# A state-space scan whose third quarter of pairs moves from VectorE to GpSimd

## The chip, the cores and the metric

The kernel runs on one core of one Trainium2 chip. The time is the device time of one execution in microseconds (us). The engines named here are TensorE (PE in the profile; PEld is its weight load), VectorE (DVE), ScalarE (ACT), GpSimd (POOL) and SyncE (SP), which issues the loads of the weights.

## The reference

Two blocks run one after the other on 256 tokens of width 2048. The second has two layers; each has a mixer, a cross attention and a feed-forward part of 8192. The change is in the mixer of its second layer, a state-space model. Cut to what matters:

```
def s5_mixer(u, lam_re, lam_im, log_dt, b_re, b_im, c_re, c_im, d_skip, w_glu, b_glu):
    lam_bar = jnp.exp(lam * dt)                       # 128 groups x 64 complex states
    def chunk_step(state, u_c):
        bu = jnp.einsum('bcgi,gpi->bcgp', u_c, b_bar)  # the input of every state
        bu = bu.at[:, 0].add(lam_bar * state)
        _, states = lax.associative_scan(combine, (a_elem, bu), axis=1)
        y = jnp.einsum('bcgp,gip->bcgi', states, c_mat).real
        return states[:, -1], y
    ...
    y = y + d_skip * uf
    z = jax.nn.gelu(y)
    return z * jax.nn.sigmoid(z @ w_glu + b_glu)
```

The mixer's input is `xn @ odd_w_in` and its result is multiplied by `odd_w_out`; both matrices and `w_glu` are 2048 x 2048.

## The kernel before

**Weights.** All large products stream their weights through a ring of 8 slots (`RING`), each 256 rows by 512 columns. For a slot, SyncE loads the raw fp32 values, ScalarE rounds them (`round_hi`, L1840: high part), VectorE subtracts (`take_lo`, L2790: low part), and TensorE takes three products for each tile (high x high, high x low, low x high; `gemm`, L988). A product waits for the counter `w_lo` of its slot, so VectorE has to keep up with the slots in the order of the program. A step of the ring is 12 matmuls. In the scan phase, `low(c, s)` is the low part for the slot eight places behind slot s of chunk c of `odd_in`; `low(3, s)` thus serves the first eight slots of the next product, `glu`.

**The scan.** The 256 tokens are taken four at a time, which leaves 64 positions. The tile `s_h` holds, on 128 partitions, 64 positions x real and imaginary x 64 pairs. The product `odd_in` makes u in four chunks (c = 0 to 3). For each, TensorE turns u (`turn_u`, L1691) and multiplies it with the input matrix (`drive`, L1707), and ScalarE copies the result into `s_h` (`driven`, L2603), which raises `bu_ready`. Chunk c gives the pairs 16c to 16c + 15. The 64 positions are scanned as 8 segments of 8: seven steps q advance all segments together (four VectorE instructions each: two products into the scratch tile `prob_t`, two additions into `s_h`), then seven steps s carry the end of one segment into the next (five instructions each). So a scan has 14 steps and 63 instructions, whatever the number of pairs. `scan(k)` is a generator that stops after each step, and its caller puts other work there. VectorE scans the pairs 0 to 15, then 16 to 31 (both on pieces of 256 elements for each partition), then 32 to 63 in one go (512 elements).

**What follows.** `scanned()` raises `scan_done` after the second scan and after the third. TensorE runs `taps` (L1733, L1739) first, which needs the tile `s_T`; GpSimd issues the four DMAs for `s_T` and two for `s_C` (L686, queue of POOL) when `odd_in` has ended. Then `read_half(0)` (L1760) waits for the first `scan_done`; ScalarE applies gelu (L2664), TensorE turns the result (`turn_z`, L1771), ScalarE copies and rounds it (L2647, L2652) and VectorE makes its low part (`z_lo`, L4132). `unread(8)` (L932) are 8 products that nobody reads. The product `glu` begins with the k range of this first half: four slots of column chunk 0, four of chunk 1. It waits for `feat_part`, which `z_lo(1)` and `z_lo(3)` raise. After its sixth slot comes `read_half(1)`, which waits for the second `scan_done`.

**Order.** The order on every engine is written by hand; each engine runs its own list from front to back. GpSimd has little work besides DMA issues and three additions on gate vectors (L762).

The line of every VectorE instruction of the scan is that of its helper, L4054.

Of the kernel before, what the change touches and what calls it, by code (L numbers as in the profile page):

```python
# [36 lines left out]
P = 128  # L37
# [4 lines left out]
CH = 512  # L42
# [12 lines left out]
PAIRS = 64  # L55
# [140 lines left out]
def two_blocks(nc, I, out):  # L196
    ctx = ExitStack()
    with ctx:
        sems = {}

        def sem(name):
            if name not in sems:
                sems[name] = ctx.enter_context(nc.semaphore(name))
            return sems[name]
# [54 lines left out]
        prob_t = sb("prob_t", [P, 2, 4, P])  # L259
# [19 lines left out]
        s_cd = dram("s_cd", (4, P, 2048))  # L279
        s_td = dram("s_td", (4, P, 1024))  # L280
# [67 lines left out]
        gemms = defaultdict(list)  # L348
# [115 lines left out]
        def groups_done(last):  # L464

            done = 0
            for st in ORDER:
                for g in gemms[st]:
                    done += g.n * g.tiles
                    if g is last:  # L470
                        return done
# [94 lines left out]
        s_T = view(4096, 32, 2, S5_STEP, 16)  # L566
        s_C = [view(o, S5_STEP, 2, 16, 16) for o in (24576, 26624, 8192, 10240)]
        s_h = view(12288, NM, 2, PAIRS)
        s_l2 = stage[:, 0, 256:512].rearrange("p (z c k) -> p z c k", z=2, c=2)
        rstd_s = stage[:, 1, 0:TT]  # L570
        S5_RUN = 8
        S5_SEGS = NM // S5_RUN
        s_pw = prob[:, :, :].rearrange("p z (r k) -> p z r k", k=PAIRS)
# [107 lines left out]
        def _(pool):  # L681
            L = Eng(pool, sem, "pool_step")

            def dma(dst, src, name):
                with nc.allow_non_contiguous_dma(reason="small constant"):
                    pool.dma_start(dst, src).then_inc(sem(name), 16)  # L686
# [28 lines left out]
            dma(x4_b1[:, 0:2], I["x"][0].rearrange("(t p) d -> p t d", p=P), "x_in")  # L715
            dma(x4_b1[:, 2:4], I["ctx"][0].rearrange("(t p) d -> p t d", p=P), "x_in")

            def flat4(v):
                return v.rearrange("p a b c d -> p (a b c d)") if len(v.shape) == 5 else v.rearrange("p a b c -> p (a b c)")

# [14 lines left out]
            for l in range(2):  # L735
                if l == 0:
                    for n, item in enumerate(b1_items[0]):
                        if item[0] == "in" and item[2] >= 6:
                            c = item[2] - 6
# [37 lines left out]
            for c in MIX:  # L777
                cs, b = mix_cols(c), c % 2
                n = cs.stop - cs.start
# [75 lines left out]
            for l in range(2):  # L855
                if l == 0:
                    pool.wait_ge(sem("mem_free"), L.due("mem_free"))
                    for j in range(2):
                        pool.wait_ge(sem(f"kv_out{j}"), 16 * 4)
                else:  # L860
                    pool.wait_ge(sem("s5_free"), L.due("s5_free"))
                    dma(s_l2.rearrange("p z c k -> p (z c k)"), s_ld2, "b_in0")
                    for j in range(2):
                        dma(flat4(s_B[j]), s_bd[j], f"b_in{j // 2}")
                    pool.wait_ge(sem("x_normed"), L.due("x_normed"))
                    dma(x_d.rearrange("(t p) d -> p t d", p=P), x4, "x_out")
                    pool.wait_ge(sem("x_out"), 32)
                    pool.wait_ge(sem("u_ready_s5"), L.due("u_ready_s5"))
                    for j in range(2, 4):
                        dma(flat4(s_B[j]), s_bd[j], f"b_in{j // 2}")  # L870
                    pool.wait_ge(sem("bu_ready"), L.due("bu_ready", 2))
                    for j in range(2):
                        dma(flat4(s_C[j]), s_cd[j], "c_in0")
                    pool.wait_ge(sem("gemm_full"), groups_done(gemms["odd"][0]))
                    for j in range(4):
                        dma(s_T[:, 8 * j:8 * j + 8].rearrange("p a b c d -> p (a b c d)"), s_td[j], "t_in_s5")
                    for j in range(2, 4):
                        dma(flat4(s_C[j]), s_cd[j], "c_in1")
                    pool.wait_ge(sem("s5_done"), L.due("s5_done"))
                    dma(x4, x_d.rearrange("(t p) d -> p t d", p=P), "dve_load")  # L880
                dma(xa_kv, kv_d[l].rearrange("(t p) d -> p t d", p=P), "mem_in")
# [932 lines left out]
        def _(act):  # L1814
# [761 lines left out]
            def odd():  # L2576
# [14 lines left out]
                def ut_in(c):  # L2591
                    for g in range(2):
                        f(s_ut[:, 8 * c:8 * c + 8, g], take_turn()[:, :].rearrange("p (n m) -> p n m", m=NM), ACT.Copy) \
                            .then_inc(sem("act_tp"), E.up("act_tp"))
                    act.wait_ge(E.last_sem(), E.last_count())
                    act.nop().then_inc(sem("ut_ready"), E.count("ut_ready"))

                def driven(c):
                    for n0 in (0, 4):
                        for o in range(2):  # L2600
                            n = 8 * c + n0
                            dst = s_h.rearrange("p m z (n o) -> p o n z m", o=2)[:, o, n:n + 4, :, 1:NM]
                            f(dst, take_turn()[:, :].rearrange("p (n z m) -> p n z m", z=2, m=NM)[:, :, :, 0:NM - 1], ACT.Copy) \  # L2603
                                .then_inc(sem("act_tp"), E.up("act_tp"))
                    act.wait_ge(E.last_sem(), E.last_count())
                    act.nop().then_inc(sem("bu_ready"), E.count("bu_ready"))
# [13 lines left out]
                def s5_ahead(c, s):  # L2620
                    if (c, s) in ((1, 3), (2, 1), (3, 1)):
                        ut_in(c - 1)
                    if (c, s) in ((1, 5), (2, 3), (3, 3)):
                        driven(c - 1)
                    if (c, s) == (2, 5):
                        for t in range(TT):
                            u_out(2, None, t, take("gemm_full"))
                    if (c, s) == (3, 6):
                        ut_in(3)
                    if (c, s) == (3, 4):  # L2630
                        for t in range(TT):
                            u_out(3, None, t, take("gemm_full"))
# [3 lines left out]
                        u_out(c, None, t, take("gemm_full"))  # L2636

                stream(g_in, u_chunk, unroll=True, each=s5_each, ahead=s5_ahead)
                driven(3)
                nonlocal g_n  # L2640
                y_at = g_n
                g_n += 4
# [72 lines left out]
        def _(dve):  # L2715
# [296 lines left out]
            def mark(name):  # L3012
                dve.wait_ge(E.last_sem(), E.last_count())
                dve.nop().then_inc(sem(name), E.count(name))
# [1025 lines left out]
            def odd():  # L4040
# [9 lines left out]
                def after(n=0):  # L4050
                    dve.wait_ge(sem("dve_step"), E.cnt["dve_step"] - n)

                def step(out, a, b, op):
                    tt(out, a, b, op).then_inc(sem("dve_step"), E.up())  # L4054

                def powers():
                    for z in range(2):
                        dve.tensor_copy(s_pw[:, z, 0], s_l2[:, z, 0]).then_inc(sem("dve_step"), E.up())
                    n = 1
                    while n < S5_RUN:  # L4060
                        after()
                        have, more = s_pw[:, :, 0:n], s_pw[:, :, n:2 * n]
                        re, im = (s_pw[:, z, n - 1].unsqueeze(1).unsqueeze(1).to_broadcast([P, 2, n, PAIRS]) for z in range(2))
                        part = prob_t[:, :, :, :].rearrange("p a b c -> p a (b c)")[:, :, 0:n * PAIRS].rearrange("p z (r k) -> p z r k", k=PAIRS)
                        step(more, have, re, ALU.mult)
                        step(part, have, im, ALU.mult)
                        after()
                        step(more[:, 0], more[:, 0], part[:, 1], ALU.subtract)
                        step(more[:, 1], more[:, 1], part[:, 0], ALU.add)
                        n *= 2  # L4070
# [37 lines left out]
                        low(c, s)  # L4108
                dve.wait_ge(sem("b_in0"), 48)
                powers()  # L4110
                nonlocal g_n, t_n
                skip("gemm_full", g_in.n * g_in.tiles)
                turn_skip(1 + 4 * 6)
# [14 lines left out]
                def z_lo(j):  # L4128
                    dve.wait_ge(sem("hi_ready"), E.due("hi_ready"))
                    ks = slice(2 * j, 2 * j + 2)  # L4130
                    name = "feat_part" if j % 2 else "dve_step"
                    tt(s_z.lo[:, ks], s_z.raw[:, ks], s_z.hi[:, ks], ALU.subtract).then_inc(sem(name), E.up(name))  # L4132

                for n, _ in enumerate(scan(slice(2 * quarter, PAIRS))):
                    if n in (1, 2):
                        low(3, n + 3)
                    if n in (7, 8):
                        z_lo(2 * n - 14)
                        z_lo(2 * n - 13)
                scanned()  # L4140
                for s in (6, 7):
                    low(3, s)
# [119 lines left out]
```

## Time and profile before

| | us |
|---|---|
| median of 3 runs | 3807.45 (3805.14 to 3809.78) |
| the profiled execution's own time | 3810.78 |
| its span, first to last instruction | 3808.8 |
| TensorE busy | 3705.3 (97%) |
| VectorE busy | 2485.9 (65%) |
| ScalarE busy | 1632.4 (43%) |
| GpSimd busy | 151.8 (4%) |

Times inside the profile count from the span's start. Busy shares are averages over all stages. The scan lies between 2752 and 2853 us. "Waits" name the engine that waited, and behind the arrow what ended its wait. The granted clock of TensorE is 1.00 at 2.4 GHz and 0.50 at 1.2 GHz; in a stretch between these it changed within it.

### The profile page before, as it was taken

To read this page: it belongs to the slowest core of one execution; us is meant where nothing else is said; L and a number is where in the kernel's file an instruction comes from. 1 tells how busy PE (TensorE), PEld (TensorE's weight loads), DVE (VectorE), ACT (ScalarE), POOL (GpSimd) and SP (SyncE) were. 2 spreads that over 40 slices of the span, in tenths; PEclk is the share of its full clock that TensorE was granted. 3 is DMA by queue.
4 is the path that set the end of the run, shared out by engine and by line. 5 is a ranking of instruction groups with operands and counts; after the bars stand their busy time and mean duration, and the time that the engine had idled before them with its cause. 6 is when DMAs were issued, how large, how long until landed. Compare 5 with 4: busy or idle time off the path is not lost.

```text
span 3808.8 us, 50649 instructions
## 1 busy us (share of the span) xinstructions
PE 3705.3 (97%) x20767; PEld 2997.6 (79%) x20767; DVE 2485.9 (65%) x3635; ACT 1632.4 (43%) x2323; POOL 151.8 (4%) x244
## 2 busy tenths in 40 slices
PE   6999999999999999999999999999989999999998
PEld 3688887787887888556888888888878888888887
DVE  7877786577776666667765645655595566545654
ACT  4422233424435443523454434444545554434443
POOL 2000000000000011022000000000000000000000
PEclk8999999999999999999999999999989999999999
DMA  9666564255863577344646656655645656556664
GB/s 376 255 210 205 184 204 170 78 177 167 270 204 111 182 244 211 103 159 145 199 153 189 192 193 189 192 191 191 237 155 162 217 156 190 192 193 189 191 204 155
DMA packets 352582, 722.46 MB, mean 190 GB/s; under 512 B 24064, under 2 KB 26436, under 8 KB 347488
## 3 DMA queue, kind: packets, MB, share of 16 engines
q1 hardware_dynamic: 331872, 637.74, 52.7%
q0 software_dynamic: 18784, 79.22, 6.0%
q8 instruction: 165, 2.70, 0.3%
q10 hardware_dynamic: 1696, 2.26, 0.2%
q14 instruction: 65, 0.53, 0.0%
HBM read 689.34 MB, written 26.37 MB: 188 GB/s over the span
## 4 chain that ended last, share of the span: by engine, by line
PE 88%; DVE 5%; DMA 3%; ACT 2%; issue 1%; POOL 1%; SPq 0%; DVEq 0%; ACTq 0%; POOLq 0%
PE acc L988 57%; PE acc L1523 6%; PE tp L1523 6%; PE acc L1521 3%; PE tp L1521 3%; PE acc L1220 3%; DMA ring<-in_w_mod 2%; PE tp L1038 2%; PE acc L1593 1%; PE acc L1093 1%; DVE big L4054 1%; DVE prob_t L4054 1%; PE acc L1076 1%; DVE ring_r L2790 1%; PE acc L906 0%
## 5 line engine op out<-in xcount | busy, mean ns | idle before, releaser
L2790 DVE TENSOR_TENSOR ring_r<-ring,ring_r 128x1024 fp32r<-128x1024 f32 (+1 forms) x984 | 1188.1, 1217 | 970.5 <-ACT ring_r L1840 959.5
L1840 ACT ACTIVATE ring_r<-ring 128x1024 fp32r<-128x1024 f32 (+1 forms) x984 | 1030.0, 1054 | 1556.9 <-DMA ring<-in_ffn_down 386.6
L988 PE MATMUL acc<-ring_r,feat_hi 128*128 128x512 f32 x2688 | 832.9, 391 | 5.2 <-DVE ring_r L2790 5.2
L988 PE MATMUL acc<-ring_r,hid_t_hi 128*128 128x512 f32 x2048 | 630.8, 389 | 0.0
L988 PEld LDWEIGHTS acc<-ring_r,feat_hi 128*128 128x128 f32 x2688 | 504.1, 188 | 116.2 <-DVE ring_r L2790 6.6
L988 PE MATMUL acc<-ring_r,feat_lo 128*128 128x512 f32 x1344 | 524.6, 390 | 0.0
L988 PEld LDWEIGHTS acc<-ring_r,hid_t_hi 128*128 128x128 f32 x2048 | 384.3, 188 | 79.3
L988 PE MATMUL acc<-ring_r,hid_t_lo 128*128 128x512 f32 x1024 | 398.4, 389 | 0.0
L1523 PE MATMUL acc<-feat_pair,ring_r 128*128 128x512 f32 x1080 | 378.9, 394 | 0.0
L1523 PE MATMUL tp<-feat_pair,ring_r 128*128 128x512 f32 x960 | 337.1, 395 | 0.0
L1521 PE MATMUL acc<-feat_pair,ring_r 128*128 128x256 f32 x1152 | 309.7, 279 | 0.3
L988 PEld LDWEIGHTS acc<-ring_r,feat_lo 128*128 128x128 f32 x1344 | 253.0, 188 | 53.3
L1521 PE MATMUL tp<-feat_pair,ring_r 128*128 128x256 f32 x1024 | 274.0, 278 | 0.0
L988 PE MATMUL acc<-ring_r,feat_e_hi 128*128 128x512 f32 (+1 forms) x832 | 247.9, 381 | 2.0 <-DVEq L2867 2.0
L1523 PEld LDWEIGHTS acc<-feat_pair,ring_r 128*128 128x128 f32 x1080 | 202.5, 188 | 43.4
L988 PEld LDWEIGHTS acc<-ring_r,hid_t_lo 128*128 128x128 f32 x1024 | 192.2, 188 | 40.1
L1521 PEld LDWEIGHTS acc<-feat_pair,ring_r 128*128 128x128 f32 x1152 | 216.5, 188 | 6.8 <-issue 0.7
L1523 PEld LDWEIGHTS tp<-feat_pair,ring_r 128*128 128x128 f32 x960 | 180.1, 188 | 39.6
L1521 PEld LDWEIGHTS tp<-feat_pair,ring_r 128*128 128x128 f32 x1024 | 192.4, 188 | 5.7
L2774 DVE SCALAR_TENSOR_TENSOR big<-ring,silu_c,big 128x512 f32<-128x512 f32 x255 | 177.4, 746 | 28.8 <-DMA ring<-in_w_mod 27.7
L988 PEld LDWEIGHTS acc<-ring_r,feat_e_hi 128*128 128x128 f32 x832 | 153.3, 188 | 32.0 <-issue 2.5
L988 PE MATMUL acc<-ring_r,feat_e_lo 128*128 128x512 f32 (+1 forms) x416 | 158.3, 381 | 0.0
(541 smaller groups left out, 4194.5 us busy)
## 6 DMA issues: line engine op xcount, KB each, us to landing
ring<-in_ffn_up SPq DMA_DIRECT2D x256, 512.0 KB, 3.7
ring<-in_ffn_down SPq DMA_DIRECT2D x256, 512.0 KB, 3.6
ring<-in_w_mod SPq DMA_DIRECT2D x192, 512.0 KB, 4.9
ring<-in_w_in SPq DMA_DIRECT2D x176, 512.0 KB, 4.0
ring<-in_w_out SPq DMA_DIRECT2D x64, 512.0 KB, 3.7
ring<-in_even_w_in SPq DMA_DIRECT2D x64, 512.0 KB, 4.5
ring<-in_xattn_wkv SPq DMA_DIRECT2D x32, 512.0 KB, 4.4
ring<-in_even_w_out SPq DMA_DIRECT2D x32, 512.0 KB, 4.2
```

What stands on the lines that cost most here:

```text
L988: mm = pe.matmul(bank[0:l.shape[-1], 0:width], l, r, start=(kk == 0 and j == 0), stop=(kk == g.kt - 1 and j == len(terms) - 1))
L1038: mm = pe.transpose(bank[0:b.shape[-1], j * P:j * P + b.shape[0]], b, ident[0:b.shape[0], 0:b.shape[0]])
L1076: pe.matmul(bank[:, 0:u["k"].shape[-1]], u["q"], u["k"], start=True, stop=True) \
L1093: mm = pe.matmul(bank[:, 0:HD], prob_t[:, (i - 2) % 2, j, :], v, start=(j == 0), stop=(j == len(u["v"]) - 1))
L1220: mm = pe.matmul(bank[:, :], mem_feat(kk)[:, t * P:(t + 1) * P], ring[:, slot, 1, k, :], start=(kk == 0), stop=(kk == g.kt - 1))
L1521: mm = pe.matmul(bank[:, 0:SEQ], w_lo, feat.hi[:, kk, :], start=False, stop=False)
L1523: mm = pe.matmul(bank[:, :], w_hi, feat_hl[:, kk, :], start=False, stop=kk == g.kt - 1)
L1593: mm = pe.matmul(x_banks[c, t][:, :], x, w, start=(kk == 0 and j == 0), stop=(kk == g_o.kt - 1 and j == 2))
L1840: f(ring_r[:, slot, 0, 0:kt, 0:width], ring[:, slot, 1, 0:kt, 0:width], ACT.Copy) \
L2774: op = stt(v, w, by, v, ALU.mult, ALU.add)
L2790: tt(lo, raw, hi, ALU.subtract).then_inc(sem("w_lo"), E.up("w_lo"))
L4054: tt(out, a, b, op).then_inc(sem("dve_step"), E.up())
```

## The change

GpSimd gets a scan of its own, with the same 14 steps, for the pairs 32 to 47. It uses the upper half of `prob_t` as scratch; VectorE uses the lower. It starts when the third `bu_ready` and the new counter `powers_ready` are there. Its DMA issues for `s_T` and the second half of `s_C`, which stood behind a wait for the end of `odd_in`, now stand behind the second of its steps. VectorE's last scan covers only the pairs 48 to 63, on pieces of 256 elements; the calls of `z_lo` in it move from steps n = 7 and 8 to n = 8 and 10, and before `scanned()` it waits for all 63 GpSimd instructions. ScalarE's `driven(3)` moves ahead of the rounding of the last slot of `odd_in`.

```
@@ gpsimd
+            def step(out, a, b, op):
+                pool.tensor_tensor(out, a, b, op).then_inc(sem("pool_step"), L.up())
+
+            def after(n=0):
+                pool.wait_ge(sem("pool_step"), L.cnt["pool_step"] - n)
+
+            def scan(k):
+                w = k.stop - k.start
+                by_run = s_h.rearrange("p (s r) c k -> p s r c k", r=S5_RUN)
+                tmp = [prob_t[:, z].rearrange("p a b -> p (a b)")[:, CH // 2:].rearrange("p (n c k) -> p n c k", n=S5_RUN, c=2)
+                       for z in range(2)]
+                for q in range(1, S5_RUN):
+                    if q > 1:
+                        after()
+                    last, h = by_run[:, :, q - 1, :, k], by_run[:, :, q, :, k]
+                    for z in range(2):
+                        step(tmp[z], last, s_l2[:, z, :, k].unsqueeze(1).to_broadcast([P, S5_SEGS, 2, w]), ALU.mult)
+                    after(1)
+                    step(h, h, tmp[0], ALU.add)
+                    after()
+                    step(h, h, tmp[1][:, :, ::-1], ALU.add)
+                    yield
...
@@ gpsimd, layer 1
-                    pool.wait_ge(sem("gemm_full"), groups_done(gemms["odd"][0]))
-                    for j in range(4):
-                        dma(s_T[:, 8 * j:8 * j + 8].rearrange("p a b c d -> p (a b c d)"), s_td[j], "t_in_s5")
-                    for j in range(2, 4):
-                        dma(flat4(s_C[j]), s_cd[j], "c_in1")
+                    pool.wait_ge(sem("bu_ready"), L.due("bu_ready"))
+                    pool.wait_ge(sem("powers_ready"), L.due("powers_ready"))
+                    for n, _ in enumerate(scan(slice(PAIRS // 2, 3 * PAIRS // 4))):
+                        if n == 1:
+                            pool.wait_ge(sem("gemm_full"), groups_done(gemms["odd"][0]))
+                            for j in range(4):
+                                dma(s_T[:, 8 * j:8 * j + 8].rearrange("p a b c d -> p (a b c d)"), s_td[j], "t_in_s5")
+                            for j in range(2, 4):
+                                dma(flat4(s_C[j]), s_cd[j], "c_in1")
@@ scalar
+                    if (c, s) == (3, 7):
+                        driven(3)
...
                 stream(g_in, u_chunk, unroll=True, each=s5_each, ahead=s5_ahead)
-                driven(3)
@@ vector
                 powers()
+                mark("powers_ready")
...
-                for n, _ in enumerate(scan(slice(2 * quarter, PAIRS))):
+                for n, _ in enumerate(scan(slice(3 * quarter, PAIRS))):
                     if n in (1, 2):
                         low(3, n + 3)
-                    if n in (7, 8):
-                        z_lo(2 * n - 14)
-                        z_lo(2 * n - 13)
+                    if n in (8, 10):
+                        z_lo(n - 8)
+                        z_lo(n - 7)
+                dve.wait_ge(sem("pool_step"), 4 * (S5_RUN - 1) + 5 * (S5_SEGS - 1))
                 scanned()
```

In the order of the instructions this is seen at two places. GpSimd before, from the first half of `s_C` (`s_cd`) to the load of x behind the mixer (`big` is the large tile that holds `s_T`, `s_C` and `s_h`):

```order
L686 DMA big<-s_cd 128x2048 [waits bu_ready]
L686 DMA big<-s_cd 128x2048
L686 DMA big<-s_td 128x1024 [waits gemm_full]
L686 DMA big<-s_td 128x1024 x3
L686 DMA big<-s_cd 128x2048 x2
L686 DMA big<-x_d 128x2x2048 [waits s5_done]
```

GpSimd after the change, from the same place to the third of its 14 steps (the other eleven follow; L719 is the new helper, `stage` holds the coefficients):

```order
L686 DMA big<-s_cd 128x2048
L719 TENSOR_TENSOR prob_t<-big,stage 128x256 [waits powers_ready,bu_ready]
L719 TENSOR_TENSOR prob_t<-big,stage 128x256
L719 TENSOR_TENSOR big<-big,prob_t 128x8x2x16 [waits pool_step] x2
L719 TENSOR_TENSOR prob_t<-big,stage 128x256 [waits pool_step]
L719 TENSOR_TENSOR prob_t<-big,stage 128x256
L719 TENSOR_TENSOR big<-big,prob_t 128x8x2x16 [waits pool_step] x2
L686 DMA big<-s_td 128x1024 [waits gemm_full]
L686 DMA big<-s_td 128x1024 x3
L686 DMA big<-s_cd 128x2048 x2
L719 TENSOR_TENSOR prob_t<-big,stage 128x256 [waits pool_step]
```

Eight additions and products now stand ahead of the loads of `s_T` (`s_td`), and 55 behind the loads.

VectorE before, from the first step of the last scan that carries a segment over to the second pair of `z_lo` (L4132):

```order
L4054 TENSOR_TENSOR prob_t<-prob,big 128x512 x2
L4054 TENSOR_TENSOR big<-big,prob_t 128x16x32
L4054 TENSOR_TENSOR big<-big,prob_t 128x8x32 x2
L4132 TENSOR_TENSOR s_zlo<-big,s_zhi 128x512 x2
L4054 TENSOR_TENSOR prob_t<-prob,big 128x512 x2
L4054 TENSOR_TENSOR big<-big,prob_t 128x16x32
L4054 TENSOR_TENSOR big<-big,prob_t 128x8x32 x2
L4132 TENSOR_TENSOR s_zlo<-big,s_zhi 128x512 x2
```

VectorE after the change, from the same step (the lines are 42 or 43 higher):

```order
L4096 TENSOR_TENSOR prob_t<-prob,big 128x256 x2
L4096 TENSOR_TENSOR big<-big,prob_t 128x16x16
L4096 TENSOR_TENSOR big<-big,prob_t 128x8x16 x2
L4096 TENSOR_TENSOR prob_t<-prob,big 128x256 x2
L4096 TENSOR_TENSOR big<-big,prob_t 128x16x16
L4096 TENSOR_TENSOR big<-big,prob_t 128x8x16 x2
L4175 TENSOR_TENSOR s_zlo<-big,s_zhi 128x512 x2
```

The pieces are half as long, and the first pair of `z_lo` stands one step later.

## Rows read from the trace of the kernel before

**Rows 1.** The page, part 4: engines in the chain that ended last.

```profile
PE 88%; DVE 5%; DMA 3%; ACT 2%; issue 1%; POOL 1%; SPq 0%; DVEq 0%; ACTq 0%; POOLq 0%
```

**Rows 2.** The page, part 1: busy time of TensorE and VectorE.

```profile
PE 3705.3 (97%) x20767; PEld 2997.6 (79%) x20767; DVE 2485.9 (65%) x3635; ACT 1632.4 (43%) x2323; POOL 151.8 (4%) x244
```

**Rows 3.** Waits of PE, 2740 to 2900: us in total, times, longest.

```profile
PE acc L988 <- DVE s_zlo L4132: 5.5, 1, 5.5
PE acc L1733 <- DMA big<-s_td: 4.1, 1, 4.1
```

**Rows 4.** Timeline of PE: start, duration, instruction, count [idle before].

```profile
2812.13 9.60 PE L1760 MATMUL acc<-big 64*64 64x64 f32 x256
...
2824.22 1.97 PE L1771 MATMUL acc<-ident,big 64*128 64x64 f32 x16 [1.34 <-ACTq L2669]
2826.12 3.78 PE L932 MATMUL acc<-ident 128*128 128x128 f32 x16
2835.40 1.19 PE L988 MATMUL acc<-ring_r,s_zhi 128*128 128x512 f32 x2 [5.51 <-DVE s_zlo L4132]
...
2840.66 0.75 PE L988 MATMUL acc<-ring_r,s_zhi 128*128 128x512 f32 x2
...
2854.52 9.64 PE L1760 MATMUL tp<-big 64*64 64x64 f32 x256
```

**Rows 5.** Busy time and granted clock (behind POOL's) in stretches.

```profile
2831.00:2835.00 4.00, 0.00 (x0) 0.00 (x0) 3.93 (x8) 0.25 (x1) 0.00 (x0) 0.50 0.00 0
...
2841.00:2843.00 2.00, 2.00 (x10) 1.63 (x9) 1.97 (x5) 0.00 (x0) 0.00 (x0) 1.00 0.45 125
```

**Rows 6.** Timeline of DVE, from the second scan to the end of the third.

```profile
2783.38 0.75 DVE L4054 TENSOR_TENSOR prob_t<-big,stage 128x256 f32<-128x256 f32 x2
2784.05 0.88 DVE L4054 TENSOR_TENSOR big<-big,prob_t 128x256 f32<-128x256 f32 x2
2784.96 0.76 DVE L4054 TENSOR_TENSOR prob_t<-big,stage 128x256 f32<-128x256 f32 x2
...
2794.49 0.76 DVE L4054 TENSOR_TENSOR prob_t<-prob,big 128x256 f32<-128x256 f32 x2
...
2806.20 4.63 DVE L2790 TENSOR_TENSOR ring_r<-ring,ring_r 128x1024 fp32r<-128x1024 f32 x4
2810.75 1.28 DVE L4054 TENSOR_TENSOR prob_t<-big,stage 128x512 f32<-128x512 f32 x2
...
2833.97 1.29 DVE L4132 TENSOR_TENSOR s_zlo<-big,s_zhi 128x512 fp32r<-128x512 f32 x2
...
2852.70 8.05 DVE L2790 TENSOR_TENSOR ring_r<-ring,ring_r 128x1024 fp32r<-128x1024 f32 x7
```

**Rows 7.** Groups of DVE by shape, 2783.3 to 2852.7: busy us, mean ns.

```profile
L4054 DVE TENSOR_TENSOR prob_t<-big,stage 128x512 f32<-128x512 f32 x14 | 9.0, 686 | 0.1
L4054 DVE TENSOR_TENSOR prob_t<-big,stage 128x256 f32<-128x256 f32 x14 | 5.3, 420 | 0.2
```

**Rows 8.** Timeline of ACT.

```profile
2780.30 3.88 ACT L2603 ACTIVATE big<-tp 128x504 f32<-128x504 f32 x4
...
2800.95 3.59 ACT L2603 ACTIVATE big<-tp 128x504 f32<-128x504 f32 x4
...
2827.32 0.63 ACT L2652 ACTIVATE s_zhi<-big 128x512 fp32r<-128x512 f32 x1
```

**Rows 9.** Timeline of POOL, around 2790.

```profile
2791.56 2.09 POOL L686 DMA_DIRECT2D big<-s_td  x4 [32.53 <-PE acc L988]
2793.64 1.05 POOL L686 DMA_DIRECT2D big<-s_cd  x2
```

**Rows 10.** Groups of POOL: busy us, mean ns.

```profile
L762 POOL TENSOR_TENSOR big<-big 128x2048 f32<-128x2048 f32 x3 | 13.5, 4521 | 14.8 <-DMA big<-in_b_mod 14.8
```

**Rows 11.** Timeline of DVE before and during a GpSimd addition (663.3 to 672.3).

```profile
661.75 0.35 DVE L2971 SCALAR_TENSOR_TENSOR big<-acc,att_s,big 128x128 f32<-128x128 f32 x1 [0.38 <-PE acc L1093]
...
666.13 0.35 DVE L2971 SCALAR_TENSOR_TENSOR big<-acc,att_s,big 128x128 f32<-128x128 f32 x1 [0.38 <-PE acc L1093]
```

More of the change, by code:

```diff
@@ L716, in _ @@
             dma(x4_b1[:, 2:4], I["ctx"][0].rearrange("(t p) d -> p t d", p=P), "x_in")
+            def step(out, a, b, op):
[18 more added lines that the diff above has]
+                    yield
+                shape = [P, S5_RUN, 2, w]
+                for s in range(1, S5_SEGS):
+                    after()
+                    end, h = by_run[:, s - 1, S5_RUN - 1, :, k].unsqueeze(1).to_broadcast(shape), by_run[:, s, :, :, k]
+                    for z in range(2):
+                        step(tmp[z], s_pw[:, z, :, k].unsqueeze(2).to_broadcast(shape), end, ALU.mult)
+                    after(1)
+                    step(h, h, tmp[0], ALU.add)
+                    after()
+                    step(h[:, :, 0], h[:, :, 0], tmp[1][:, :, 1], ALU.subtract)
+                    step(h[:, :, 1], h[:, :, 1], tmp[1][:, :, 0], ALU.add)
+                    yield
+                after()
             def flat4(v):
```

## The prediction, made before the changed kernel ran

> **What bounds the kernel now.** I read part 4 of the page first, the chain that ended last. TensorE holds 88% of it and VectorE 5% [rows 1], and TensorE is busy 97% of the span [rows 2]. So the change is worth what it takes from TensorE's idle time or adds to it; VectorE's 65% decide nothing by themselves.
>
> The waits of TensorE in the scan phase come next [rows 3]. It waits twice: 4.1 us for the load of `s_T`, and 5.5 us for `s_zlo`, the low part by VectorE. The timelines show why the second is there. ScalarE begins the second rounding at 2827.32 and needs 0.63 us [rows 8], so both operands of `z_lo(1)` are there at 2827.95. TensorE ends its unread products at 2826.12 + 3.78 = 2829.90. But VectorE is inside the scan of 32 pairs and comes to `z_lo` only at 2833.97 [rows 6]; TensorE starts `glu` at 2835.40 [rows 4]. The idle time also costs clock: the granted clock is 0.50 in 2831 to 2835 and 1.00 from 2841 [rows 5]. The first 12 matmuls of `glu` take 2840.66 - 2835.40 = 5.26 us [rows 4]. The 60 that follow up to 2854.52 take 13.86 us, 0.23 us each, at which pace 12 take 2.8 us. So this place costs up to 5.5 + 2.5 = 8.0 us, and that is all that a faster scan can give: `read_half(1)` follows at 2854.52 without a wait, because the second `scan_done` is there at 2852.7 [rows 4, 6]. Behind it TensorE is full, and what is gained or lost at `glu` reaches the end one for one.
>
> **What is removed.** VectorE's third scan works on 512 elements for each instruction, 0.686 us; on 256 it is 0.420 us [rows 7]. That gives 0.266 us for 256 elements (1.04 ns each) and 0.154 us that doesn't depend on the size. A q step on 256 elements takes 2784.96 - 2783.38 = 1.58 us, an s step 1.66 (2794.49 and the next; the second scan ends at 2806.20, seven steps after 2794.49, which is 1.67) [rows 6]. The last scan begins at 2810.75 either way. After the change `z_lo(1)` would be done behind 7 x 1.58 + 2 x 1.66 + two `low` of 4.63 / 4 = 1.15 + two `z_lo` of 0.65: 11.1 + 3.3 + 2.3 + 1.3 = 18.0 us, so at 2828.8, before TensorE wants it at 2829.9. The scan itself ends after five more s steps and two more `z_lo`, 9.6 us, at 2838.4. TensorE would come to `read_half(1)` at 2854.52 - 8.0 = 2846.5.
>
> **What is added.** 63 GpSimd instructions, 49 on 256 elements and 14 on 128. The trace has GpSimd additions only on 2048 elements: 4.521 us, 2.2 ns for an element [rows 10]. In proportion, 256 elements cost 0.565 us; with VectorE's fixed 0.154 us, 0.72. I take 0.72 (and 0.44 for the short ones), because a short instruction has a start too: 49 x 0.72 + 14 x 0.44 = 41.4 us. GpSimd starts when the third `driven` ends, 2780.30 + 3.88 = 2784.2 [rows 8]; `powers_ready` is long there. With 3.1 us of DMA issues [rows 9] it ends at 2828.8, 17.7 us before TensorE asks. It would be late only above (2846.5 - 2784.2 - 3.1) / 63 = 0.94 us for an instruction.
>
> **The moved DMA issues.** The loads of `s_T` go behind eight GpSimd instructions: 2784.2 + 8 x 0.72 = 2790.0, and they waited for the end of `odd_in` until 2791.56 anyway [rows 9]. Nothing at 0.72; at 0.94 us the loads start 0.2 us late, and TensorE's wait for `s_T` grows by as much. The 2 issues for `s_C` are needed at 2854 only. The long queue on GpSimd behind them holds `dma(x4)` after the mixer, which is far away.
>
> **The new wait on VectorE.** Behind the wait for the 63 instructions stand `scan_done`, `low(3, 6)`, `low(3, 7)` and the lows of `glu`. TensorE needs these only after `read_half(1)`, 9.64 us long [rows 4], and before the change they also started at the end of the scan [rows 6]. So only the time of `scan_done` matters.
>
> **ScalarE.** `driven(3)` before the last rounding (about 1 us) ends at about 2802.5 in place of 2804.5 [rows 8]. VectorE asks for it at 2810.75 [rows 6], `low(3, 7)` later still. Nothing.
>
> **The disputed cost: both engines on SBUF at once.** If they run freely, the sum is -5.5 - 2.5 = -8.0 us. But from 2784.2 on VectorE has hardly a gap, and every instruction of both reads two operands from SBUF. The only overlap in this trace is with softmax work: a VectorE instruction that reads PSUM and one SBUF tile takes 0.35 us both before and inside a GpSimd addition [rows 11]. That is no slowdown, but it isn't this pair: there VectorE reads one operand from SBUF. So the cost is bounded by free overlap and by full exclusion, where an instruction of one holds the other back. By exclusion in turns, only the data parts excluding each other, a pair of long instructions takes 0.266 + 0.565 = 0.83 us, a short pair 0.42. VectorE has 61 of the 63 instructions of its second scan left at 2784.2, 47 long and 14 short, 0.74 us for an average pair. Eight run beside the DMA issues (3.1 us), 53 in pairs: 39 us. The first `scan_done` comes at 2826.4 in place of 2806.2. Four `low` (4.6 us) lose 2.3 us to the next four GpSimd instructions, the last scan 3 us to the remaining six: `z_lo(1)` ends at 2826.4 + 6.9 + 18.0 + 3.0 = 2854.3, and `glu` starts 19.0 us later than before, with `read_half(1)` not late. With whole durations excluding each other (0.35 + 0.66 = 1.01 us for a pair) the same sum gives +33. If VectorE always goes first, its chain keeps its times and GpSimd is starved: between packed data parts without a gap (VectorE 96 x 0.266 + 28 x 0.133 for the scans + 6 x 1.06 for `low` + 4 x 0.53 for `z_lo` = 38 us, GpSimd 49 x 0.565 + 14 x 0.28 = 32 us: the second `scan_done` at about 2854, -1 us in all) and everything after 2838.4 (+28).
>
> I take exclusion in turns, +19 us. The nearest row leans to free overlap, but with another kind of instruction. What decides for me is the asymmetry: VectorE's chain from 2784.2 to `z_lo(1)` has 6.6 us of slack against the old 2835.4 and 2.5 us of clock. That is 16 stalls of 0.565 us; if more than a quarter of the 63 GpSimd instructions hold VectorE up, the gain is gone.
>
> The Trainium skill, page "SBUF — State Buffer", section "Who interferes with whom", says that a VectorE instruction with two SBUF inputs contends with a GpSimd instruction that reads SBUF: one of them blocks for the whole instruction. By it the sum is the +19 to +33 above; without it -8. No row here shows it; rows 11 don't contradict it.
>
> **Rivals.**
> *Free overlap.* For it: rows 11, and the work is independent (other pairs, other scratch). Against it: no row with two operands on each side. -5.5 us of wait and up to -2.5 of clock: 3810.78 - 8.0 = 3802.8 in the profiled execution, 3799.5 in the median. If the clock comes back late the gain is only 5.5.
> *GpSimd is slow by itself.* No exclusion, but the short strided pieces cost it more than in proportion. It decides from 0.94 us for an instruction; at 1.2 us it ends at 2784.2 + 75.6 + 3.1 = 2862.9, TensorE waits at `read_half(1)` from 2846.5 to 2863: +8, 3815.5. VectorE's durations stay 0.42, the wait moves from `glu` to `read_half(1)`. Nearest row against it: 2.2 ns for an element [rows 10].
> *The scan wasn't late.* If TensorE's wait at `glu` were not for the scan, nothing would change. Against it: its operands were there 6.0 us before 2833.97 [rows 6, 8]. I give it nothing of its own.
>
> **How the numbers follow.** The sums stand against the profiled 3810.78, 3.3 us above the median of 3807.45; I shift the median by them. Exclusion: 0.54, nearly all of it slower (0.52 slower, 0.02 within). Free overlap: 0.36; its -8.0 is just at the bound of 0.2%, 7.6 us, below which a measurement of this kernel can't tell a change from none, so 0.22 faster, 0.14 within. Slow GpSimd: 0.10, from -4 to +8 and more: 0.04 within, 0.06 slower. Together faster 0.22, within 0.20, slower 0.58. The time is that of exclusion in turns, 3807.45 + 19 = 3826.5. Its own range is +5 to +33. The range of the whole goes from free overlap with a little more gain (-9) to +28: 3798 to 3836.
>
> **What would show it.** Right: VectorE's 256-element instructions between 2784 and 2840 well above 0.42 us (0.8 or more, waits included) and the first `scan_done` behind 2820, with TensorE idle before `read_half(0)` and `glu`. Right in the bookkeeping in any case: the loads of `s_T` issued within 1 us of the old time, GpSimd's first product at 2784. Wrong: VectorE's instructions at 0.42 us beside GpSimd's; then TensorE has no wait before `glu`, the clock is at 1.00 soon after 2830, and the kernel is 5 to 8 us faster. GpSimd instructions above 0.94 us with VectorE at 0.42 would show the third case.

## The result and the profile after

| | before | changed kernel |
|---|---|---|
| median, us | 3807.93 (3805.14 to 3809.78, 4 runs) | 3829.51 (3829.14 to 3830.33, 4 runs) |
| profiled execution, us | 3810.78 | 3829.14 |
| its span, us | 3808.8 | 3827.2 |

The changed kernel is slower by a factor of 1.0057, 95% interval 1.0045 to 1.0070. The medians differ by 21.6 us, the two profiled executions by 18.4 us, because the profiled one of before lay 3 us above its median.

The three longest waits of TensorE's matmuls between 2740 and 2900 in the changed kernel (us in total, times, longest; the lines are higher by 41 to 43 than those of [rows 3]):

```profile
PE acc L1801 <- issue: 16.7, 1, 16.7
PE acc L1029 <- DVE s_zlo L4175: 9.7, 1, 9.7
PE acc L1774 <- DMA big<-s_td: 3.8, 1, 3.8
```

The wait for `s_T` is 3.8 us, about what it was (4.1 before). The wait for `z_lo` at `glu` has grown from 5.5 to 9.7 us, and there is a new one of 16.7 us at `read_half(0)` (L1801). The profile names no releaser for it; VectorE's timeline shows it. Here it is for the second scan, the four `low` and the last scan (start, duration, instruction, count):

```profile
2783.25 0.75 DVE L4096 TENSOR_TENSOR prob_t<-big,stage 128x256 f32<-128x256 f32 x2
2783.92 1.30 DVE L4096 TENSOR_TENSOR big<-big,prob_t 128x256 f32<-128x256 f32 x2
2785.26 1.73 DVE L4096 TENSOR_TENSOR prob_t<-big,stage 128x256 f32<-128x256 f32 x2
2786.91 1.83 DVE L4096 TENSOR_TENSOR big<-big,prob_t 128x256 f32<-128x256 f32 x2
...
2791.89 0.76 DVE L4096 TENSOR_TENSOR prob_t<-big,stage 128x256 f32<-128x256 f32 x2
2792.57 0.88 DVE L4096 TENSOR_TENSOR big<-big,prob_t 128x256 f32<-128x256 f32 x2
...
2796.53 1.72 DVE L4096 TENSOR_TENSOR prob_t<-big,stage 128x256 f32<-128x256 f32 x2
...
2800.01 1.68 DVE L4096 TENSOR_TENSOR prob_t<-big,stage 128x256 f32<-128x256 f32 x2
...
2828.94 6.07 DVE L2832 TENSOR_TENSOR ring_r<-ring,ring_r 128x1024 fp32r<-128x1024 f32 x4
2834.92 1.60 DVE L4096 TENSOR_TENSOR prob_t<-big,stage 128x256 f32<-128x256 f32 x2
...
2854.24 1.29 DVE L4175 TENSOR_TENSOR s_zlo<-big,s_zhi 128x512 fp32r<-128x512 f32 x2
...
2864.91 4.63 DVE L2832 TENSOR_TENSOR ring_r<-ring,ring_r 128x1024 fp32r<-128x1024 f32 x4
```

And GpSimd's, rows between its start and its end:

```profile
2783.92 1.90 POOL L719 TENSOR_TENSOR prob_t<-big,stage 128x256 f32<-128x256 f32 x2 [25.19 <-ACTq L2647]
2785.78 1.81 POOL L719 TENSOR_TENSOR big<-big,prob_t 128x256 f32<-128x256 f32 x2
...
2791.28 2.16 POOL L686 DMA_DIRECT2D big<-s_td  x4 [0.15 <-issue]
2793.42 1.05 POOL L686 DMA_DIRECT2D big<-s_cd  x2
...
2838.63 2.14 POOL L719 TENSOR_TENSOR big<-big,prob_t 128x256 f32<-128x256 f32 x3
```

A pair of VectorE's independent products takes 0.75 us until GpSimd starts at 2783.92, then 1.73. While GpSimd issues DMAs (2791.28 to 2794.47) it is back at 0.76. Afterwards a q step takes 2800.01 - 2796.53 = 3.48 us, where it took 1.58 [rows 6]: 0.87 us for one instruction of each engine. The second scan ends at 2828.8 in place of 2806.2, TensorE's `read_half(0)` starts at 2829.09 in place of 2812.13, `glu` at 2855.68 in place of 2835.40 and `read_half(1)` at 2873.76 in place of 2854.52 [rows 4]. GpSimd is done at 2840.8, VectorE's last scan at 2864.9, so the new wait for the 63 instructions holds nobody. Behind `read_half(1)` little changes: it is 19.2 us later by these times, and the profiled executions differ by 18.4.

The end of these rows stands at a slightly different distance from the start in every execution: the powers' first copy, ahead of the scans, is at 2747.66 in the profile of before, at 2747.39 after, and between 2742 and 2748 in the experiments. Where times of several traces are compared below, they are taken from that copy: `glu` starts 87.7 us behind it before, `read_half(1)` 106.9 us; in the changed kernel 108.3 and 126.4, so +20.6 and +19.5.

### The profile page after: what moved, and what is told of

Read it like the earlier page. It is cut to its first block, busy times and chain, and to the rows that moved or that the text cites. A ratio compares the mean times of both kernels' runs of the same rounds, so it can differ in the third digit from the quotient of the medians.

```text
span 3827.2 us, 50715 instructions
## 1 busy us (share of the span) xinstructions
PE 3705.8 (97%) x20767; PEld 2998.1 (78%) x20767; DVE 2499.7 (65%) x3635; ACT 1633.5 (43%) x2323; POOL 203.7 (5%) x307
## 4 chain that ended last, share of the span: by engine, by line
PE 89%; DVE 5%; DMA 3%; ACT 2%; issue 1%; POOL 1%; SPq 0%; DVEq 0%; ACTq 0%; POOLq 0%
PE acc L1029 57%; PE acc L1564 6%; PE tp L1564 6%; PE acc L1562 3%; PE tp L1562 3%; PE acc L1261 3%; PE tp L1079 2%; DMA ring<-in_w_mod 2%; DVE big L4096 1%; PE acc L1634 1%; DVE prob_t L4096 1%; PE acc L1134 1%; PE acc L1117 1%; DVE ring_r L2832 1%; PE acc L947 1%
```

## The experiments

### Without the third quarter: what the change would have given

The GpSimd scan and VectorE's wait for it are taken out; the rest of the change stays.

```
-                    for n, _ in enumerate(scan(slice(PAIRS // 2, 3 * PAIRS // 4))):
-                        if n == 1:
-                            pool.wait_ge(sem("gemm_full"), groups_done(gemms["odd"][0]))
+                    pool.wait_ge(sem("gemm_full"), groups_done(gemms["odd"][0]))
...
-                dve.wait_ge(sem("pool_step"), 4 * (S5_RUN - 1) + 5 * (S5_SEGS - 1))
```

> The changed kernel, but the third quarter of the pairs (32 to 47) is scanned by nobody: GpSimd's 63 instructions and VectorE's wait for them are left out, so that part of the result is not computed. This is what the change would give if GpSimd's work cost VectorE nothing. Theory A (the two engines exclude each other, and this alone makes the changed kernel slow): VectorE's 256-element instructions at 0.42 us, first scan_done at 2806, glu from 2829.9 without a wait, read_half(1) at 2846.5; 8.0 us faster than before (3799.5), so 29 us are the price of the exclusion. Theory B (the moved DMA issues, driven(3) or the new places of z_lo cost something themselves): less than 5 us faster, with a wait of TensorE at s_T or glu that is longer than before.

Measured: 3799.43 us against 3807.15, ratio 0.9979 (0.9968 to 0.9990), so 4 to 12 us faster. The two longest waits of TensorE in this run:

```profile
PE acc L1772 <- DMA big<-s_td: 4.3, 1, 4.3
PE acc L1810 <- ACTq L2709: 1.3, 1, 1.3
```

The wait at `glu` is gone, the one at `s_T` is as before. `glu` starts 82.0 us behind the copy (5.7 earlier than before) and `read_half(1)` 99.3 (7.6 earlier). VectorE is at 0.42 us again (the row covers 2783.3 to 2840):

```profile
L4094 DVE TENSOR_TENSOR prob_t<-big,stage 128x256 f32<-128x256 f32 x21 | 8.0, 419 | 0.2
```

So the forecast of 8.0 us for a scan that costs VectorE nothing holds (7.7), and no price of the rest of the change can be seen (theory B falls). The price of GpSimd's scan is 3829.51 - 3799.43 = 30 us by the two medians; measured each against its own runs of the kernel before, it is 21.6 + 7.7 = 29 us, the forecast of this run.

### GpSimd behind VectorE: its own speed

GpSimd starts when VectorE has ended its last scan.

```
-                    for n, _ in enumerate(scan(slice(PAIRS // 2, 3 * PAIRS // 4))):
-                        if n == 1:
-                            pool.wait_ge(sem("gemm_full"), groups_done(gemms["odd"][0]))
+                    pool.wait_ge(sem("gemm_full"), groups_done(gemms["odd"][0]))
...
+                    pool.wait_ge(sem("powers_ready"), 2)
+                    for _ in scan(slice(PAIRS // 2, 3 * PAIRS // 4)):
+                        pass
...
+                after()
+                mark("powers_ready")
                 dve.wait_ge(sem("pool_step"), 4 * (S5_RUN - 1) + 5 * (S5_SEGS - 1))
```

> The changed kernel, but GpSimd starts its scan only when VectorE has ended its last one (2838), and VectorE is idle meanwhile. Everything is computed. Theory A: GpSimd's instructions alone take 0.65 to 0.72 us on 256 elements and 0.36 to 0.44 on 128 (0.87 to 0.97 and 0.62 in the changed kernel), 38 to 42 us for all 63; VectorE's are all at 0.42 us, the first scan_done is at 2806 and glu starts at 2829.9 as in the run without the third quarter; read_half(1) waits until about 2878, so some 24 us slower than before. Theory C (GpSimd is slow by itself on these short strided pieces, and VectorE doesn't matter to it): its instructions stay at 0.87 to 0.97 us, 52 us for all, read_half(1) at 2890, 36 us slower.

Measured: 3835.39 us, one run. GpSimd's groups (busy us, mean ns), first here, alone:

```profile
L719 POOL TENSOR_TENSOR big<-big,prob_t 128x256 f32<-128x256 f32 x21 | 15.1, 719 | 0.5
L719 POOL TENSOR_TENSOR prob_t<-prob,big 128x256 f32<-128x256 f32 x14 | 9.7, 717 | 0.5
L719 POOL TENSOR_TENSOR big<-big,prob_t 128x128 f32<-128x128 f32 x14 | 6.0, 450 | 0.6
```

then in the changed kernel, beside VectorE:

```profile
L719 POOL TENSOR_TENSOR big<-big,prob_t 128x256 f32<-128x256 f32 x21 | 18.4, 878 | 0.6
L719 POOL TENSOR_TENSOR prob_t<-prob,big 128x256 f32<-128x256 f32 x14 | 13.2, 966 | 0.5
L719 POOL TENSOR_TENSOR big<-big,prob_t 128x128 f32<-128x128 f32 x14 | 8.4, 624 | 0.6
```

GpSimd by itself is no slower than the 0.72 and 0.44 us of the prediction; the whole scan takes 2879.4 - 2837.1 = 42.3 us. Theory C falls. An estimate from the same numbers of what a GpSimd instruction of this kind is made of: (0.719 - 0.450) / 128 = 2.10 ns for an element and 0.18 us besides. `read_half(1)` waits 35.1 us for it and comes 27.3 us later than before; expected were 24. `glu` starts 82.5 us behind the copy, undisturbed.

### GpSimd reads one operand, then none

```
             def step(out, a, b, op):
-                pool.tensor_tensor(out, a, b, op).then_inc(sem("pool_step"), L.up())
+                one = pool.tensor_copy(out, a) if L.cnt["pool_step"] < 4 * (S5_RUN - 1) else pool.memset(out, 0.0)
+                one.then_inc(sem("pool_step"), L.up())
```

> The changed kernel, but the 28 GpSimd instructions of its q steps copy their first operand (one SBUF input) and the 35 of its s steps write zeros (no input); the third quarter is therefore not scanned rightly. Waits and counts are the same. Theory A (what collides are reads of SBUF): VectorE is held beside the copies, by less than beside the additions (0.2 to 0.4 us each), and not at all beside the writes of zeros, where it is at 0.42 us. Theory D (any GpSimd instruction, or its semaphore traffic, holds VectorE up): VectorE is above 0.5 us in both parts.

VectorE's timeline, beside the copies (the first four rows) and beside the writes of zeros (the last two; GpSimd's zeros start at 2805.80 and end at 2814.7):

```profile
2796.68 1.04 DVE L4097 TENSOR_TENSOR prob_t<-prob,big 128x256 f32<-128x256 f32 x2
2797.64 1.21 DVE L4097 TENSOR_TENSOR big<-big,prob_t 128x256 f32<-128x256 f32 x3
2798.89 1.04 DVE L4097 TENSOR_TENSOR prob_t<-prob,big 128x256 f32<-128x256 f32 x2
2799.85 1.22 DVE L4097 TENSOR_TENSOR big<-big,prob_t 128x256 f32<-128x256 f32 x3
...
2807.25 0.76 DVE L4097 TENSOR_TENSOR prob_t<-prob,big 128x256 f32<-128x256 f32 x2
2807.93 0.94 DVE L4097 TENSOR_TENSOR big<-big,prob_t 128x256 f32<-128x256 f32 x3
```

GpSimd's copy rows there and a row of its zeros:

```profile
2797.93 1.19 POOL L719 COPY big<-big 128x256 f32<-128x256 f32 x2
2799.18 1.01 POOL L719 COPY prob_t<-big 128x256 f32<-128x256 f32 x2
...
2807.08 0.57 POOL L719 MEMSET prob_t<- 128x256 f32 x2
```

Beside the copies an s step takes 2798.89 - 2796.68 = 2.21 us in place of 1.66, 0.11 us more for each of its five instructions; I had written 0.2 to 0.4. GpSimd makes only four copies in that time (its q step takes 2799.18 - 2796.97 = 2.21 us), so one copy holds VectorE up by 0.14 us. Beside the zeros an s step takes 1.65 us, as it does alone. Theory D (any GpSimd instruction) falls: it is its reads that hold VectorE. The single time, 3807.09 us against 3807.15, has nothing to tell apart here; in the trace `read_half(1)` is 3.6 us earlier than before.

### VectorE reads one operand, then none

```
...
+                    elif light[0] == 1:
+                        one = ts(out, a, 0.5, None, ALU.mult)
+                    else:
+                        one = dve.memset(out, 0.0)
...
+                light[0] = 1
+                for n, _ in enumerate(scan(slice(quarter, 2 * quarter))):
+                    if n == S5_RUN - 2:
+                        light[0] = 2
```

> The changed kernel, but in VectorE's second scan (pairs 16 to 31) the 28 instructions of the q steps multiply one SBUF operand by a constant and the 35 of the s steps write zeros; that quarter is therefore not scanned rightly. GpSimd's instructions are the additions and products of the changed kernel. Theory A: beside VectorE's zeros GpSimd is at its own speed (0.65 to 0.72 us on 256 elements) and VectorE is not held; the same beside the one-operand products, unless these take the second way to SBUF too. Theory D (it is not the second operand, but that both work on SBUF at once): both are held as in the changed kernel (GpSimd 0.87 us and more).

VectorE's rows: two products alone, four beside GpSimd's instructions, two during its DMA issues, then zeros beside its additions, and last the four `low`:

```profile
2783.57 0.49 DVE L2781 TENSOR_SCALAR prob_t<-big 128x256 f32<-128x256 f32 x2
...
2786.00 1.65 DVE L2781 TENSOR_SCALAR big<-big 128x256 f32<-128x256 f32 x2
2787.68 1.53 DVE L2781 TENSOR_SCALAR prob_t<-big 128x256 f32<-128x256 f32 x2
...
2792.41 0.61 DVE L2781 TENSOR_SCALAR big<-big 128x256 f32<-128x256 f32 x2
...
2800.95 0.55 DVE L4103 MEMSET prob_t<- 128x256 f32 x2
...
2807.67 6.24 DVE L2832 TENSOR_TENSOR ring_r<-ring,ring_r 128x1024 fp32r<-128x1024 f32 x4
```

and GpSimd's beside the zeros (first row) and beside the four `low` (the last two):

```profile
2802.40 1.54 POOL L719 TENSOR_TENSOR big<-big,prob_t 128x256 f32<-128x256 f32 x2
...
2807.01 2.48 POOL L719 TENSOR_TENSOR prob_t<-big,stage 128x256 f32<-128x256 f32 x2
2809.45 3.37 POOL L719 TENSOR_TENSOR big<-big,prob_t 128x256 f32<-128x256 f32 x2
```

Beside VectorE's zeros GpSimd is at its own speed: two additions in 1.54 us (1.51 alone). The zeros show no stall either: all their s steps take 1.33 to 1.34 us, wherever GpSimd's instructions fall. Beside the `low`, with 1024 elements and two operands, GpSimd waits too: 3.37 us for two, and the four `low` take 6.24 us in place of 4.63. The exclusion goes both ways. It isn't a matter of a shared tile: the `low` read `ring` and `ring_r`, GpSimd `big`, `prob_t` and `stage`. The one-operand products are held as well: 1.65 us for two, 0.61 alone. That isn't the softmax instruction of [rows 11], which also read one operand from SBUF but the other from PSUM and lost nothing. The product by a constant is fast, 0.28 us for 256 elements by the profile (two in 0.49 us, since the second starts before the first has ended). If 0.15 us of it don't depend on the size, as with the two-operand instruction, 0.13 us are left for the data, half of the 0.27 us there; that it uses a second way to SBUF for this, and is held up for that reason, is only inferred. Theory A holds for the zeros, and for the products only with the reservation made in it. The time of the single run is 3820.04 us; its VectorE is still held up in the `low` and in the last scan.

### An eighth of the pairs

GpSimd scans the pairs 32 to 39, VectorE's last scan 40 to 63. GpSimd's scratch shrinks to the last quarter of each half of `prob_t`, since VectorE's needs more.

```
-                tmp = [prob_t[:, z].rearrange("p a b -> p (a b)")[:, CH // 2:].rearrange("p (n c k) -> p n c k", n=S5_RUN, c=2)
+                tmp = [prob_t[:, z].rearrange("p a b -> p (a b)")[:, 3 * CH // 4:].rearrange("p (n c k) -> p n c k", n=S5_RUN, c=2)
...
-                    for n, _ in enumerate(scan(slice(PAIRS // 2, 3 * PAIRS // 4))):
+                    for n, _ in enumerate(scan(slice(PAIRS // 2, 5 * PAIRS // 8))):
...
-                for n, _ in enumerate(scan(slice(3 * quarter, PAIRS))):
+                for n, _ in enumerate(scan(slice(5 * PAIRS // 8, PAIRS))):
```

> The changed kernel, but GpSimd scans only the pairs 32 to 39 (128 elements for each instruction) and VectorE's last scan the pairs 40 to 63 (384 elements). Everything is computed. Theory A (in turns, the data parts exclude each other): a pair of long instructions takes 0.27 + 0.28 + 0.05 = 0.60 us beside the second scan in place of 0.88; the first scan_done is at about 2815 (2806 before, 2829 in the changed kernel), four low and the wider last scan (2.05 us for a step) put z_lo(1) at 2846, glu starts 11 us later than before, the kernel is 8 to 13 us slower than before. Theory E (each GpSimd instruction costs VectorE the same, whatever its size, since the count decides): still 63 of them, so the first scan_done stays at 2826 or later and the kernel is 20 us slower or more.

Measured: 3818.07 us against 3808.19, ratio 1.0027 (1.0017 to 1.0038): +9.9 us, inside the 8 to 13. VectorE in its second scan: the starts of two q steps beside GpSimd's q steps, and then one s step and the start of the next:

```profile
2781.51 1.17 DVE L4096 TENSOR_TENSOR prob_t<-big,stage 128x256 f32<-128x256 f32 x2
...
2783.92 1.17 DVE L4096 TENSOR_TENSOR prob_t<-big,stage 128x256 f32<-128x256 f32 x2
...
2796.08 1.15 DVE L4096 TENSOR_TENSOR prob_t<-prob,big 128x256 f32<-128x256 f32 x2
2797.15 1.33 DVE L4096 TENSOR_TENSOR big<-big,prob_t 128x256 f32<-128x256 f32 x3
2798.52 1.15 DVE L4096 TENSOR_TENSOR prob_t<-prob,big 128x256 f32<-128x256 f32 x2
```

The q step of four takes 2.41 us, 0.60 us for one instruction of each engine as expected (0.87 in the changed kernel). The s step of five takes 2.44 us (3.6 in the changed kernel, 1.66 alone). So the price goes with the size of GpSimd's instructions and not with their number (theory E falls). Counted from the copy, the first `scan_done` comes 8.6 us later than before, `glu` 10.1 and `read_half(1)` 9.0. That also holds the wider last scan on VectorE.

### ScalarE's edit alone, and z_lo alone

`driven(3)` ahead of the last rounding, in the kernel before:

```
+                    if (c, s) == (3, 7):
+                        driven(3)
...
                 stream(g_in, u_chunk, unroll=True, each=s5_each, ahead=s5_ahead)
-                driven(3)
```

> The kernel before, with driven(3) ahead of the last slot's rounding as the only change. It isn't on the path: VectorE asks for the third quarter's inputs at 2810.75 and they are there at 2804.5 before and 2802.5 now. Theory A: no change, within 3 us of before, the waits of TensorE at s_T (4.1) and z_lo (5.5) as they were. Theory B (this edit has a price or a gain of its own): more than 4 us either way.

Measured: 3807.46 against 3808.19, ratio 1.0001 (0.9992 to 1.0010): no change. TensorE's waits are 4.8 us at `s_T` and 5.0 us at `z_lo`, together within 0.2 us of before.

The places of `z_lo`, in the kernel before:

```
-                    if n in (7, 8):
-                        z_lo(2 * n - 14)
-                        z_lo(2 * n - 13)
+                    if n in (5, 7):
+                        z_lo(n - 5)
+                        z_lo(n - 4)
```

> The kernel before, with z_lo(0), z_lo(1) behind step n = 5 of the last scan and z_lo(2), z_lo(3) behind n = 7 (7 and 8 before); nothing else. z_lo(1) then ends at 2830.0, and TensorE starts glu at 2830 with the clock back at once: the wait of 5.5 us at glu is gone. But VectorE's last scan still ends at 2852.7, and TensorE would be at read_half(1) at 2846.5, so it waits there for 6 us. Expected: 1 to 2 us faster than before, no more. A rival (only the wait at glu and its clock count) would have it 8 us faster.

Measured: 3806.04 against 3808.19, ratio 0.9999 (0.9990 to 1.0008; the two medians alone would give 0.9994, inside it): no change that can be told, and not 8 us, which would be 0.9979. TensorE's wait has moved:

```profile
PE tp L1760 <- DVEq L4101: 5.0, 1, 5.0
PE acc L1733 <- DMA big<-s_td: 4.9, 1, 4.9
```

The 5.5 us at `glu` are now 5.0 us at `read_half(1)`. In the trace `read_half(1)` is 1.8 us earlier than before, as expected. So the 8 us can be had only if VectorE's last scan ends earlier too.

### Two scans on VectorE in place of three

```
-                dve.wait_ge(sem("bu_ready"), E.due("bu_ready"))
-                for n, _ in enumerate(scan(slice(0, quarter))):
-                    if n % 2 and n // 2 < g_in.slots:
-                        low(2, n // 2)
-                low(2, g_in.slots - 1)
-                dve.wait_ge(sem("bu_ready"), E.due("bu_ready"))
-                for _ in scan(slice(quarter, 2 * quarter)):
-                    pass
+                low(2, 0)
+                dve.wait_ge(sem("bu_ready"), E.due("bu_ready", 2))
+                for n, _ in enumerate(scan(slice(0, 2 * quarter))):
+                    if n + 1 < g_in.slots:
+                        low(2, n + 1)
...
-                    if n in (7, 8):
-                        z_lo(2 * n - 14)
-                        z_lo(2 * n - 13)
+                    if n in (6, 7):
+                        z_lo(2 * n - 12)
+                        z_lo(2 * n - 11)
```

> The kernel before with two scans on VectorE in place of three: pairs 0 to 31 in one scan (512 elements for each instruction), which starts when the second bu_ready is there (2757.6, in place of 2752.4 for the first quarter), then 32 to 63; low(2, 0) stands ahead of the first scan, the others behind its steps 0 to 6, and z_lo(0..3) behind n = 6 and 7 of the last scan. Everything is computed. One scan on 512 elements costs 37.6 us where two on 256 cost 45, and it starts 5.3 us later: the first scan_done comes at 2803.5 in place of 2806.2, the last scan ends at about 2850 in place of 2852.7, glu starts at 2830 without a wait, read_half(1) at 2850. Expected: 4 us faster than before. If a low(2, n) comes too late for TensorE in the last chunk of odd_in, there is a wait of TensorE on w_lo before 2791 that wasn't there, and the gain shrinks.

Measured: 3804.55 us (11 runs) against 3808.19 (31 runs), ratio 0.9988 (0.9980 to 0.9997). It is faster than both kernels; against the one before the gain is 0.03 to 0.20%. TensorE's three longest waits:

```profile
PE acc L1733 <- DMA big<-s_td: 4.0, 1, 4.0
PE acc L988 <- DVE s_zlo L4129: 2.0, 1, 2.0
PE tp L1760 <- DVEq L4101: 1.8, 1, 1.8
```

The 5.5 us have become 2.0 + 1.8, and `read_half(1)` is 3.5 us earlier; 4 us were expected. The 2.0 us at `glu` had not been expected: `z_lo(1)` behind n = 6 comes a little late. The low parts did not come too late; VectorE idles 6.2 us ahead of the first scan instead of doing two narrow ones.

## Why the prediction was right

The forecast was +19 us with exclusion in turns as the likeliest, and its steps stand against the trace as follows.

- *The ceiling.* 8.0 us for a scan that costs VectorE nothing: 7.7 us in the run without the third quarter. Its trace has 5.7 us for the wait at `glu` and 1.9 us up to `read_half(1)` for the clock; the forecast had 5.5 and 2.5. The clock wasn't back at once: the granted clock was 0.50 in the first 1.4 us of `glu` and 0.98 behind them.
- *GpSimd's price.* 0.72 us for 256 elements and 0.44 for 128, taken as the proportional part of a long instruction [rows 10] and VectorE's fixed part: 0.72 and 0.45 alone. 41.4 us for all: 42.3.
- *The pair.* 0.83 us for a long pair from the data parts alone, 0.74 for an average: 0.87 measured for a long one. The engines wait for each other's data part and for about 0.04 us more, and not for whole instructions, with which the same long pair would take 0.40 + 0.72 = 1.12 us (the prediction's 1.01 us is for the average pair). That was the choice that put the sum at +19 and not +33. It stood on no row of before; the runs bear it out.
- *The first scan_done.* 2826.4 forecast, 2828.8 measured. The four `low` took 6.0 us, not 6.9; the last scan up to `z_lo(1)` 20.6 us, not 21.0. These errors, +2.4, -0.9 and -0.4 us, partly cancel: `z_lo(1)` ended at 2855.5, forecast 2854.3; `glu` started 20.3 us later by the page's times (20.6 from the copy), forecast 19.0.
- *read_half(1).* +19.2 by the page's times, 19.5 from the copy: a little less than at `glu`, since in the changed kernel the clock was low for the first 9 matmuls of `glu` (0.53 in 2855.7 to 2859.3, 1.00 from 2859.4) and before for the first 12 (0.50 in 2835.4 to 2840.6).
- *The end.* The medians differ by 21.6 us, 2 us more than `read_half(1)` and 3 more than the profiled executions. The prediction's step from `glu` to the end, one for one, is right within that; whether the 2 us are only the spread of the runs is not shown.
- *The cheap edits.* The loads of `s_T` were issued at 2791.28 (2791.56 before), GpSimd's first product started at 2783.92, `driven(3)` alone is worth nothing.

The step with the least ground in the profile was the exclusion itself, at 0.54. The runs settle it. GpSimd alone is at its own speed, VectorE without GpSimd's scan at its own, and together they hold each other up when both read SBUF; GpSimd's writes of zeros and VectorE's writes of zeros hold nobody. The Trainium skill's page "SBUF — State Buffer", section "Who interferes with whom", says that a VectorE instruction with two SBUF inputs contends with GpSimd instructions that read SBUF and not with one that only writes. The traces agree (0.87 us for a pair beside additions, 0.42 for VectorE beside zeros). Its section "SBUF: two separate sides" says that the loser blocks for the whole instruction. Here one stall is 0.87 - 0.40 = 0.47 us for a GpSimd instruction of 0.72, so less than its whole duration.

What the prediction did not see is the wait at `read_half(0)`, 16.7 us, as a place of its own: it named the late `scan_done` but summed only at `glu`. The sum is the same, since TensorE has to wait for `z_lo(1)` afterwards anyway (9.7 us), and VectorE's list decides when that comes.

## What to carry to other kernels

An idle GpSimd is no free second VectorE: while both read two operands from SBUF they take turns. Here an element costs 2.1 ns on GpSimd and 1.04 on VectorE, and a pair of instructions takes the sum of both. A stretch in which VectorE is idle or only writes left GpSimd at its own speed in these runs, and a VectorE instruction with one operand in PSUM was not held up [rows 11]; elementwise work is better moved there, though no run here tried it. When an engine is late for two consumers in a row, removing the first wait moves it to the second (5.5 us became 5.0 us at the next place): ask how much shorter the engine's whole list must be. Here the shorter list came from fewer, wider instructions.

## What the runs showed of the hardware

- GpSimd, two SBUF operands in fp32, alone: 0.719 us for 256 elements, 0.450 for 128, 4.521 for 2048.
- VectorE and GpSimd, 256 elements with two operands each: one of both in 0.87 us, in turns. With GpSimd at 128 elements: 0.60 us, and 2.44 us for an s step of five VectorE instructions, where alone they take 1.66.
- VectorE's product with a constant on 256 elements takes 0.28 us alone and 0.8 beside GpSimd's products and additions; one operand from SBUF is thus no protection, one from SBUF and one from PSUM was [rows 11].
- One GpSimd copy of 256 elements holds VectorE's two-operand instructions up by 0.14 us, its memset and its DMA issues not at all.
